# Gathering and put-back of tokens moved between half products, and four conditioning strips moved to an earlier stage

## Chip, cores and metric

One Trainium2 chip, one core. The metric is the device time of one execution in microseconds. The kernel is one program written out engine by engine (TensorE "PE", VectorE "DVE", ScalarE "ACT", GpSimd "POOL", SyncE "SP"), which meet only at semaphores.

## What is computed

256 tokens of 1024 features, float32. Two blocks in a row:

```
# first block
h = mixer(x)                 # four branches a (linear recurrence), b (gated delta rule),
                             # c (stick-breaking attention), d (gated linear attention);
merged = sum_n sigmoid(merge_in_n) * (y_n @ w_branch[n]);  h = merged @ w_out
x = layer_norm(2**0.25 * x + h)
scores -> best of 4 groups of 4 experts -> 2 experts of that group
y = sum_e combine[e] * ((silu(x @ w_gate[e]) * (x @ w_up[e])) @ w_down[e])
x = layer_norm(2**0.25 * x + y)
# second block, two layers
for i in 0, 1:
    mod = silu(c) @ ada_w[i] + ada_b[i]          # 1024 x 9216: shifts, scales, gates
    x = x + .5*g0*rmsnorm(swiglu(modulate(rmsnorm(x)), 1024 x 2752))
    x = x + g1*rmsnorm(attention_i(modulate(rmsnorm(x))))   # 0: sparse, 1: differential
    x = x + .5*g2*rmsnorm(swiglu(modulate(rmsnorm(x)), 1024 x 2752))
```

## The kernel before

**Weights.** SP loads every weight in units of 1 MB into a ring of six slots (L494 to L506). Unit n+6 is issued when unit n is released, by a count that PE or another engine raises after the last use of its slot. In the expert stage and in the feed-forward products each unit is split in two parts for precise products: ACT writes `w_hi` (`high_at`, L1703), DVE writes `w_lo` = weight less `w_hi` (`low_at`, L2409), and each product is three matmuls (`mm3`).

**First mixer.** The order of work on all engines comes from one list, `STEPS`. `d_gate` is the gates of branch d: eight matmuls on PE, then a chain of exponentials, logarithms and one scan on ACT and DVE (L1620, L2142) that ends in `d_q`; `d_attn` on PE (L850) waits for it. Between them stand merge steps 8 and 9. A merge step is the product of one 128-column gate tile and its branch tile; two of them share a unit of `w_in`, four a unit of `w_branch`, and DVE releases three units after every fourth step (L2292).

**Conditioning strips.** The product `silu(c) @ ada_w[i]` is a filler: 36 units a layer, in five quads, each a sum in one PSUM bank. A quad of eight units writes four rows at partitions 0, 32, 64, 96 (columns in four groups); the last quad, of four units, writes two. `p_ada` (L1009) makes one unit's share; when a quad is complete ACT copies it to `ada_row` (`ada_drain`, L1534) and POOL stores it (`store_quad`, L591). There is one `ada_row`, so a drain waits for the store before it. Layer one's strips (here number 0) lie in the first mixer and ahead of the experts; all 36 of layer two lie in sparse attention, as `fill(count)`: 3 + 5 before the index products, 8 within them, 8 behind them, and 2, 2, 2, 2, 1, 1, 1, 1 in the eight softmax iterations (L1380).

**Expert stage.** Tokens are sorted by group into five tiles of 128 slots; each tile passes its group's four experts, 20 runs in all. A run s is, on PE (`experts`, L1218): turn the hidden rows of run s-1 (`turn_hidden`, PSUM bank 4), two half products with `w_gate`, two with `w_up`, two with `w_down` of run s-1; a half product is 12 matmuls of 512 columns. In the run with e = 2 the next tile's tokens are gathered in four pieces (`gather`: eight small matmuls, taken out of PSUM by ACT's `sorted_rows`); in the run with e = 1 the finished tile is put back in four pieces (`scatter`: two matmuls, added to `acc`, which is `merged` in the profile, by DVE's `y_add`). All pieces of both use PSUM bank 7, one after the other. A put-back needs the tile's output split in two parts: ACT's `y_high`, then DVE's `y_low`, which raises `y_split`. DVE's order in a run is: `y_low` if putting back, `hid_lo` (raises `run_hT`), adds 0 to 2, `w_lo` of both `w_down` halves and of the next `w_gate` half 0, `run_h`, add 3, the other three `w_lo`.

## Time and profile before

| | us |
|---|---|
| median of 3 runs | 2211.09 (2205.53 to 2212.61) |
| profiled execution | 2211.7 |
| its span, first to last instruction | 2210.0 |
| PE busy | 2071.6 |
| DVE busy | 1188.6 |
| ACT busy | 903.0 |
| mean granted clock of PE | 0.945 |

The span is what the rows below add up to; 1.7 us of the profiled execution lie around it. PE's matmuls are recorded with their pipelined length, so that a busy PE says that matmuls follow each other, not at which rate: the distance between starts gives the rate. A time in brackets behind an instruction is the idle time of its engine before it, with what ended it. PEclk is the granted clock as a share of full speed: 1.00 is 2.4 GHz and 0.50 is 1.2 GHz.

### The profile page before, as it was taken

What the parts mean: (1) busy time and instruction counts of PE and PEld (TensorE: products, weight loads), DVE (VectorE), ACT (ScalarE), POOL (GpSimd) and SP (SyncE); (2) the same over time, 40 slices, a digit from 0 to 9 for tenths busy, and PEclk for the clock granted to TensorE, in tenths of its full rate; (3) what the DMA queues carried; (4) which work ended last, traced back from release to release, by engine and by line L of the source; (5) the groups of instructions that cost most, each with busy time, mean ns of one, the idle gap of its engine ahead of it and who ended that gap; (6) DMA issues with size and microseconds to landing.
All of it is one profiled execution on the core that took longest, in us unless ns stands there. A gap on an engine that the chain in (4) does not pass through costs nothing.

```text
span 2210.0 us, 29686 instructions
## 1 busy us (share of the span) xinstructions
PE 2071.6 (94%) x12013; PEld 1723.7 (78%) x12013; DVE 1188.6 (54%) x1686; ACT 903.0 (41%) x1300; POOL 60.7 (3%) x144
## 2 busy tenths in 40 slices
PE   8999989989979999998899997899999999879998
PEld 6777778787547777776899972489999999847997
DVE  2060353441269878878655646455566555455544
ACT  1132520111047776775443433443344335454333
POOL 5000000000000000000000000000000000000000
PEclk9999986987989999999899997999999999979999
DMA  6875220302589988898355679546655655403652
GB/s 220 283 265 180 94 98 17 103 13 95 203 332 336 327 324 309 311 355 302 129 183 184 199 274 419 194 139 205 195 185 173 199 180 191 153 20 114 205 194 95
DMA packets 207241, 441.81 MB, mean 200 GB/s; under 512 B 8108, under 2 KB 158732, under 8 KB 183584
## 3 DMA queue, kind: packets, MB, share of 16 engines
q1 hardware_dynamic: 201568, 424.70, 55.3%
q0 software_dynamic: 5568, 15.67, 2.1%
q8 instruction: 72, 1.18, 0.2%
q14 instruction: 33, 0.27, 0.0%
HBM read 439.14 MB, written 1.20 MB: 199 GB/s over the span
## 4 chain that ended last, share of the span: by engine, by line
PE 65%; DVE 6%; ACT 4%; DMA 4%; issue 1%; SPq 0%; ACTq 0%; DVEq 0%
PE P L672 64%; DMA ring<-in_ada_w 1%; DMA ring<-in_w_down 1%; ACT merged L1482 1%; DVE w_lo L2018 1%; DVE w_lo L2413 1%; DMA ring<-in_w_up 1%; ACT w_hi L1707 1%; DVE h L1971 1%; DMA ring<-in_w_gate 1%; DVE xs L1971 1%; DVE xs L1964 0%; ACT pT L1482 0%; DVE y_lo L1964 0%; ACT st L1482 0%
## 5 line engine op out<-in xcount | busy, mean ns | idle before, releaser
L672 PE MATMUL P<-x_parts,w_hi 128*128 128x256 f32 x2560 | 458.2, 281 | 2.1 <-DVE w_lo L2018 2.1
L672 PEld LDWEIGHTS P<-x_parts,w_hi 128*128 128x128 f32 x2560 | 399.0, 189 | 8.9 <-DVE w_lo L2018 2.8
L2018 DVE TENSOR_TENSOR w_lo<-ring,w_hi 128x1024 fp32r<-128x1024 f32 x302 | 351.5, 1220 | 79.6 <-ACT w_hi L1514 79.4
L672 PE MATMUL P<-w_hi,x_parts 128*128 128x256 f32 (+2 forms) x1504 | 375.7, 336 | 3.2 <-DVE w_lo L2413 3.2
L672 PE MATMUL P<-x_parts,w_lo 128*128 128x256 f32 x1280 | 361.2, 282 | 0.0
L1514 ACT ACTIVATE w_hi<-ring 128x1024 fp32r<-128x1024 f32 x302 | 297.4, 1050 | 52.1 <-DMA ring<-in_ffn_w_down 48.8
L2413 DVE TENSOR_TENSOR w_lo<-ring,w_hi 128x1024 fp32r<-128x1024 f32 x240 | 279.2, 1221 | 27.3 <-ACT w_hi L1707 25.4
L672 PEld LDWEIGHTS P<-w_hi,x_parts 128*128 128x128 f32 x1504 | 262.0, 194 | 32.4 <-issue 4.1
L1707 ACT ACTIVATE w_hi<-ring 128x1024 fp32r<-128x1024 f32 x240 | 240.5, 1052 | 105.2 <-DMA ring<-in_w_up 39.8
L672 PE MATMUL P<-xT,ring 128*128 128x256 f32 x1152 | 267.4, 389 | 4.5 <-ACT xT L1482 3.1
L672 PEld LDWEIGHTS P<-xT,ring 128*128 128x128 f32 x1152 | 222.6, 196 | 50.7 <-issue 20.2
L672 PEld LDWEIGHTS P<-x_parts,w_lo 128*128 128x128 f32 x1280 | 241.7, 189 | 0.0
L672 PE MATMUL P<-w_lo,x_parts 128*128 128x256 f32 (+2 forms) x752 | 238.4, 338 | 0.0
L672 PE MATMUL P<-w_hi,hid_hi 128*128 128x512 f32 x512 | 202.7, 396 | 1.7 <-DVE hid_lo L1964 1.4
L672 PE MATMUL P<-w_lo,hid_hi 128*128 128x512 f32 x512 | 204.2, 399 | 0.0
L672 PE MATMUL P<-w_hi,hid_lo 128*128 128x512 f32 x512 | 201.0, 392 | 0.0
L1698 ACT ACTIVATE silu<-P 128x256 f32<-128x256 f32 x88 | 33.7, 383 | 371.1 <-PE P L672 352.3
L2398 DVE TENSOR_TENSOR hid<-silu,P 128x256 f32<-128x256 f32 (+1 forms) x80 | 33.7, 421 | 251.1 <-ACT silu L1698 250.2
L672 PEld LDWEIGHTS P<-w_lo,x_parts 128*128 128x128 f32 x752 | 146.5, 195 | 12.7 <-issue 0.5
L672 PEld LDWEIGHTS P<-w_hi,hid_hi 128*128 128x128 f32 x512 | 96.4, 188 | 24.3 <-issue 1.9
L672 PEld LDWEIGHTS P<-w_hi,hid_lo 128*128 128x128 f32 x512 | 96.2, 188 | 22.7
L672 PEld LDWEIGHTS P<-w_lo,hid_hi 128*128 128x128 f32 x512 | 96.1, 188 | 17.9
(439 smaller groups left out, 2044.9 us busy)
## 6 DMA issues: line engine op xcount, KB each, us to landing
ring<-in_ada_w SPq DMA_DIRECT2D x72, 1024.0 KB, 8.9
ring<-in_ffn_w_gate SPq DMA_DIRECT2D x44, 1024.0 KB, 5.5
ring<-in_ffn_w_up SPq DMA_DIRECT2D x44, 1024.0 KB, 8.0
ring<-in_ffn_w_down SPq DMA_DIRECT2D x44, 1024.0 KB, 4.9
ring<-in_w_in SPq DMA_DIRECT2D x40, 1024.0 KB, 7.3
ring<-in_w_gate SPq DMA_DIRECT2D x40, 1024.0 KB, 4.9
ring<-in_w_up SPq DMA_DIRECT2D x40, 1024.0 KB, 4.9
ring<-in_w_down SPq DMA_DIRECT2D x40, 1024.0 KB, 5.1
```

The source lines that it names most:

```text
L672: return pe.matmul(o, l, r, start=start, stop=stop, **kw)
L1482: a.done(act.activation(o, i, fn, **kw), name)
L1514: act.activation(w_hi[:, slot, c:c + half], ring[:, slot, c:c + half], ACT.Copy).then_inc(sem("w_hi"), 1)
L1698: act.activation(silu[:, k % 2, :], P[:, k % 2, 0:S], ACT.Silu).then_inc(sem("silu"), 1)
L1707: act.activation(w_hi[:, n % R, c:c + UNIT // 2], ring[:, n % R, c:c + UNIT // 2], ACT.Copy).then_inc(sem("w_hi"), 1)
L1971: v.done(dve.scalar_tensor_tensor(out=o, in0=x, scalar=s, in1=y, op0=op0, op1=op1), name)
L2018: dve.tensor_tensor(w_lo[:, slot, c:c + half], ring[:, slot, c:c + half], w_hi[:, slot, c:c + half].bitcast(F32), ALU.subtract).then_inc(s ...
L2398: dve.tensor_tensor(x, silu[done:128, k % 2, :], P[done:128, k % 2, S:2 * S], ALU.mult).then_inc(sem("hid_part"), 1)
L2413: dve.tensor_tensor(w_lo[:, n % R, c:c + UNIT // 2], ring[:, n % R, c:c + UNIT // 2], w_hi[:, n % R, c:c + UNIT // 2].bitcast(F32), ALU.su ...
```

## The change

Five edits, of which the first two go together:

- **Four strips of layer two** (the last quad, now first in that layer's order) go from the softmax iterations of sparse attention into the first mixer, between `b_pre` and merge step 8, with their four 1 MB loads, one ACT drain and one POOL store. `d_attn` waits for the drain too, since it uses the same bank (7). The softmax iterations keep one strip each. `DRAINS` is the new order of drains over both layers.
- Waits, counts and the list of loads follow from that. The merge units of the ring are listed step by step, which is the same order as before apart from the four new ones.
- **Gathering** alternates between banks 7 and 4: pieces 0 to 3 stand behind half products gate 0, gate 1, up 0, up 1 as before, but piece q waits for the copy of piece q-2 and no more of q-1. Pieces 1 and 3 use the bank of `turn_hidden`, so piece 1 waits for `run_hT`, and the next run begins with a wait for all four copies. ACT copies pieces 1 and 2 one after the other behind `silu`, and piece 3 behind the next split.
- **Put-back** moves each piece one half product later: behind gate 1, up 0, up 1 and down 0.
- **DVE's order**: the adds 0, 1, 2, 3 stand behind `w_lo` of `w_down` half 0, of `w_down` half 1, behind `run_h`, and behind `w_lo` of the next `w_gate` half 1.

```diff
-QUADS = (2, 3, 4, 0, 1), (0, 1, 2, 3, 4)
-BANKS = (6, 7, 6, 0, 1), (6, 7, 6, 7, 6)
+QUADS = (2, 3, 4, 0, 1), (4, 0, 1, 2, 3)
+BANKS = (6, 7, 6, 0, 1), (7, 6, 7, 6, 7)
...
+NEXT_ADA = len(QUAD_UNITS[QUADS[1][0]])
+DRAINS = [(0, k) for k in range(EARLY)] + [(1, 0)] + [(0, k) for k in range(EARLY, ADA_QUADS)] + [(1, k) for k in range(1, ADA_QUADS)]
...
-STEPS += [("d_gate",), ("b_pre",), _MERGE[8], _MERGE[9], ("d_attn",), _MERGE[10], ("d_intra",)]
+STEPS += [("d_gate",), ("b_pre",)] + [("ada", n, 1) for n in range(NEXT_ADA)]
+STEPS += [_MERGE[8], _MERGE[9], ("d_attn",), _MERGE[10], ("d_intra",)]
...
             for k in range(EARLY):
                 store_quad(0, k)
+            store_quad(1, 0)
...
             def p_d_attn():
                 t.see("d_q")
                 pe.wait_ge(sem("y2"), 4)
+                pe.wait_ge(sem("ada_out"), DRAINS.index((1, 0)) + 1)
...
+                    if e == 3 and k + 1 < TILES:
+                        pe.wait_ge(sem("x_taken"), 4 * k + 8)
...
                         t.tell(wide_half("w_gate", s, 0, s % 2), "half_used")
                         if gathering:
                             if k:
                                 pe.wait_ge(sem("y_added"), 4 * k)
                             gather(k + 1, 0, 7)
+                        t.tell(wide_half("w_gate", s, 1, s % 2), "gate_out")
                         if scattering:
                             pe.wait_ge(sem("y_split"), k)
                             scatter(k - 1, 0, 7)
-                        t.tell(wide_half("w_gate", s, 1, s % 2), "gate_out")
+                        if gathering:
+                            pe.wait_ge(sem("run_hT"), s)
+                            gather(k + 1, 1, 4)
+                        t.tell(wide_half("w_up", s, 0, 2 + s % 2), "half_used")
+                        if gathering:
+                            pe.wait_ge(sem("x_taken"), 4 * k + 5)
+                            gather(k + 1, 2, 7)
                         if scattering:
                             pe.wait_ge(sem("y_added"), 4 * (k - 1) + 1)
                             scatter(k - 1, 1, 7)
-                        if gathering:
-                            pe.wait_ge(sem("x_taken"), 4 * k + 5)
-                            gather(k + 1, 1, 7)
-                        t.tell(wide_half("w_up", s, 0, 2 + s % 2), "half_used")
-                        if gathering:
-                            pe.wait_ge(sem("x_taken"), 4 * k + 6)
-                            gather(k + 1, 2, 7)
+                        t.tell(wide_half("w_up", s, 1, 2 + s % 2), "up_out")
                         if scattering:
                             pe.wait_ge(sem("y_added"), 4 * (k - 1) + 2)
                             scatter(k - 1, 2, 7)
-                        t.tell(wide_half("w_up", s, 1, 2 + s % 2), "up_out")
-                        if scattering:
-                            pe.wait_ge(sem("y_added"), 4 * (k - 1) + 3)
-                            scatter(k - 1, 3, 7)
                         if gathering:
-                            pe.wait_ge(sem("x_taken"), 4 * k + 7)
-                            gather(k + 1, 3, 7)
+                            pe.wait_ge(sem("x_taken"), 4 * k + 6)
+                            gather(k + 1, 3, 4)
...
                         t.tell(down_half(s - 1, 0), "half_used")
+                        if scattering and s < RUNS:
+                            pe.wait_ge(sem("y_added"), 4 * (k - 1) + 3)
+                            scatter(k - 1, 3, 7)
...
-                    fill((2, 2, 2, 2, 1, 1, 1, 1)[n])
+                    fill(1)
...
                         f(run_silu, P[:, s % 2, :], ACT.Silu, "run_silu")
                         if gathering:
-                            sorted_rows(k + 1, 1, 7)
+                            sorted_rows(k + 1, 1, 4)
+                            sorted_rows(k + 1, 2, 7)
                         if s + 1 < RUNS:
                             high_at(expert_at["w_gate", s + 1, 1])
                         if gathering:
-                            sorted_rows(k + 1, 2, 7)
+                            sorted_rows(k + 1, 3, 4)
...
-                        if scattering:
-                            for b in range(3):
-                                y_add(b, 7)
                     if 0 < s < RUNS:
                         low_at(expert_at["w_down", s - 1, 0])
+                        if scattering:
+                            y_add(0, 7)
                         low_at(expert_at["w_down", s - 1, 1])
+                        if scattering:
+                            y_add(1, 7)
...
                     if scattering:
+                        y_add(2, 7)
+                    if s + 1 < RUNS:
+                        low_at(expert_at["w_gate", s + 1, 1])
+                    if scattering:
                         y_add(3, 7)
```

## Rows read from the trace of the kernel before

**Rows 1.** The page, its parts 1 and 4: busy time, and the chain of waits.
```profile
PE 2071.6 (94%) x12013; PEld 1723.7 (78%) x12013; DVE 1188.6 (54%) x1686; ACT 903.0 (41%) x1300; POOL 60.7 (3%) x144
...
PE 65%; DVE 6%; ACT 4%; DMA 4%; issue 1%; SPq 0%; ACTq 0%; DVEq 0%
```

**Rows 2.** Waits of PE, 660 to 1032 us: waiter, releaser, us in total, times, longest.
```profile
PE P L672 <- DVE y_lo L1964: 6.5, 4, 2.9
PE P L672 <- ACT x_parts L1482: 4.1, 6, 1.6
```

**Rows 3.** Timeline of PE, expert stage: start, length, engine, line, operation, [idle before].
```profile
797.37 0.63 PE L1196 MATMUL P<-ident,hid 128*128 128x128 f32 x4
...
814.64 0.63 PE L1196 MATMUL P<-ident,hid 128*128 128x128 f32 x4
...
819.80 0.51 PE L672 MATMUL P<-y_hi,to_token 128*128 128x512 f32 x1 [1.77 <-DVE y_lo L1964]
...
820.38 0.39 PE L672 MATMUL P<-w_hi,x_parts 128*128 128x512 f32 x1
...
824.71 0.39 PE L672 MATMUL P<-y_hi,to_token 128*128 128x512 f32 x1
...
837.59 0.63 PE L1196 MATMUL P<-ident,hid 128*128 128x128 f32 x4
...
846.27 0.66 PE L672 MATMUL P<-to_slot,rows_hi 128*128 128x128 f32 x4 [1.58 <-ACT x_parts L1482]
```

**Rows 4.** Stretches: busy time of each engine, PEclk, DMA share, GB/s.
```profile
820.00:825.00 5.00, 5.00 (x16) 3.91 (x16) 1.16 (x2) 4.68 (x6) 0.00 (x0) 0.66 0.42 177
846.00:852.00 6.00, 5.73 (x24) 4.81 (x25) 6.00 (x6) 5.31 (x7) 0.00 (x0) 0.72 0.41 160
```

**Rows 5.** Waits of DVE 815 to 838 us; its timeline there and in the run behind.
```profile
DVE merged L1964 <- PE P L672: 6.9, 3, 4.1
...
818.34 1.41 DVE L1964 TENSOR_TENSOR y_lo<-P,y_hi 128x512 fp32r<-128x512 f32 x2
...
829.45 6.90 DVE L2413 TENSOR_TENSOR w_lo<-ring,w_hi 128x1024 fp32r<-128x1024 f32 x6
...
844.59 0.68 DVE L1964 TENSOR_TENSOR hid_lo<-P,hid_hi 128x512 fp32r<-128x512 f32 x1
```

**Rows 6.** Timeline of ACT, the run with gathering.
```profile
843.73 2.00 ACT L1707 ACTIVATE w_hi<-ring 128x1024 fp32r<-128x1024 f32 x2 [1.66 <-DMA ring<-in_w_down]
845.64 0.58 ACT L1482 ACTIVATE x_parts<-P 128x512 fp32r<-128x512 f32 x1
```

**Rows 7.** Timeline of PE and DVE, the gates' wait of the first mixer.
```profile
285.63 3.72 PE L672 MATMUL P<-xT,ring 128*128 128x256 f32 x16
...
294.37 1.89 PE L672 MATMUL P<-yT,ring 128*128 128x256 f32 x8
...
305.16 3.77 PE L672 MATMUL P<-gl_q,gl_k 128*128 128x128 f32 x16 [8.90 <-DVE gl_k L1964]
...
309.64 3.62 PE L672 MATMUL P<-xT,ring 128*128 128x256 f32 x16
...
308.11 0.42 DVE L1964 TENSOR_TENSOR merged<-merged,tmpm 128x256 f32<-128x256 f32 x1
```

**Rows 8.** Landing of the two loads of w_in issued at 284.0 and 284.5 us.
```profile
DMA to landing us min/median/max: 7.7/9.6/11.4
```

**Rows 9.** Timeline of PE, strips of a four-group quad and of the last quad.
```profile
150.76 1.04 PE L672 MATMUL P<-ring,cols 128*1 128x512 f32 x8
...
185.59 1.88 PE L672 MATMUL P<-ring,cols 128*1 128x512 f32 x8
```

**Rows 10.** Timeline of PE, sparse attention: last strip before the scores, first iterations.
```profile
1355.91 1.88 PE L672 MATMUL P<-ring,cols 128*1 128x512 f32 x8 [0.59 <-DMA ring<-in_ada_w]
...
1363.07 3.59 PE L672 MATMUL P<-ring,cols 128*1 128x512 f32 x16
```

**Rows 11.** Waits of ACT, the softmax iterations, 1366 to 1404 us.
```profile
ACT pT L1482 <- PE P L1387: 7.1, 6, 2.5
```

More of the change, by code:

```diff
@@ L168, in weight_loads @@
             out.append(projections.pop(0))
-        elif step == "ada":
-            ada(0, which[0])
-    for b in BRANCH_ORDER:
-        for half in range(2):
-            out.append((w_branch[b][:, half * 512:half * 512 + 512].rearrange("(t p) n -> p t n", p=128),
-                        4, 512, 128))
-            cols(w_in, C_MERGE + b * D + half * 512, 512)
+        elif step == "merge":
+            b, d = BRANCH_ORDER[which[0] // DT], which[0] % DT
+            if d % 4 == 0:
+                out.append((w_branch[b][:, d * 128:d * 128 + 512].rearrange("(t p) n -> p t n", p=128), 4, 512, 128))
+            if d % 2 == 0:
+                cols(w_in, C_MERGE + b * D + d * 128, 256)
+        elif step == "ada":
+            ada(which[1] if len(which) > 1 else 0, which[0])
     square(A["w_out"][0])
@@ L187, in weight_loads @@
                 if layer == 0:
-                    for n in range(ADA_UNITS):
+                    for n in range(NEXT_ADA, ADA_UNITS):
                         ada(1, n)
@@ L276, in quad_ends @@
     def quad_ends(layer, k):
-        return ADA_UNITS * layer + sum(len(QUAD_UNITS[q]) for q in QUADS[layer][:k + 1])
+        return sum(len(QUAD_UNITS[QUADS[l][j]]) for l, j in DRAINS[:DRAINS.index((layer, k)) + 1])
     with ctx:
@@ L449, in build @@
         SPARSE_WIDTHS = [256] * (A_IN // 256) + [A_IN % 256]
-        ATTENTION_UNITS = {"sparse": -(-A_IN // 256) + ADA_UNITS + D // 256, "differential": DIFF_IN // 256 + D // 256, "ffn": 0}
+        ATTENTION_UNITS = {"sparse": -(-A_IN // 256) + ADA_UNITS - NEXT_ADA + D // 256, "differential": DIFF_IN // 256 + D // 256, "ffn": 0}
         def out_bank(n):
@@ L593, in store_quad @@
                 rows, p = raw_rows(layer, QUADS[layer][k])
-                pool.wait_ge(sem("ada_out"), ADA_QUADS * layer + k + 1)
+                pool.wait_ge(sem("ada_out"), DRAINS.index((layer, k)) + 1)
                 pool.dma_start(rows, ada_row[0:p:32, :]).then_inc(sem("ada_stored"), 16)
             def load_modr(layer):
-                pool.wait_ge(sem("ada_stored"), 16 * ADA_QUADS * (layer + 1))
+                pool.wait_ge(sem("ada_stored"), 16 * (1 + DRAINS.index((layer, ADA_QUADS - 1))))
                 load(modr[:, layer, :], mod_raw[layer].rearrange("(p q) -> p q", q=128), "modr_here")
@@ L653, in _ @@
                 if n == 1:
-                    for k in range(ADA_QUADS):
+                    for k in range(1, ADA_QUADS):
                         store_quad(1, k)
@@ L1017, in p_ada @@
                     t.see("cond")
-                if d == 0 and k >= 2:
-                    pe.wait_ge(sem("ada_out"), ADA_QUADS * layer + k - 1)
+                if d == 0:
+                    earlier = [m for m, (l, j) in enumerate(DRAINS[:DRAINS.index((layer, k))]) if BANKS[l][j] == BANKS[layer][k]]
+                    if earlier:
+                        pe.wait_ge(sem("ada_out"), earlier[-1] + 1)
                 for dd in range(w.shape[1]):
@@ L1238, in experts @@
                         else:
-                            pe.wait_ge(sem("ada_out"), EARLY + s + 1)
+                            pe.wait_ge(sem("ada_out"), DRAINS.index((0, EARLY + s)) + 1)
                         t.tell(wide_half("w_gate", s, 0, s % 2), "half_used")
@@ L1330, in fill @@
                     for _ in range(count):
-                        k = filled[0]
+                        k = NEXT_ADA + filled[0]
                         filled[0] += 1
@@ L1536, in ada_drain, with a_ada @@
                 act.wait_ge(sem("ada_used"), quad_ends(layer, k))
-                if layer + k:
-                    act.wait_ge(sem("ada_stored"), 16 * (ADA_QUADS * layer + k))
+                before = DRAINS.index((layer, k))
+                if before:
+                    act.wait_ge(sem("ada_stored"), 16 * before)
                 p = 128 if QUADS[layer][k] < 4 else 64
                 f(ada_row[0:p, :], P[0:p, BANKS[layer][k], :], ACT.Copy, "ada_out")
-            def a_ada(n):
+            def a_ada(n, layer=0):
+                if layer:
+                    if n + 1 == NEXT_ADA:
+                        ada_drain(1, 0)
+                    return
                 for k in range(EARLY):
@@ L1769, in a_experts @@
                                 high_at(expert_at["w_up", s + 1, half])
-                        if gathering:
-                            sorted_rows(k + 1, 3, 7)
                         if s == RUNS - 1:
@@ L2473, in v_experts @@
                     if scattering:
+                        y_add(2, 7)
+                    if s + 1 < RUNS:
+                        low_at(expert_at["w_gate", s + 1, 1])
+                    if scattering:
                         y_add(3, 7)
                     if s + 1 < RUNS:
-                        low_at(expert_at["w_gate", s + 1, 1])
                         low_at(expert_at["w_up", s + 1, 0])
```

2 lines of the change are left out of this document (removed).

## The prediction

> **What bounds the kernel now.** I read the page first [rows 1]: PE is busy 94% of the span and makes up 65% of the chain that ended last; no other engine has more than 6%. So a part of the change is worth what it takes off PE's waits or PE's own work, and where PE waits for another engine, what is left of that engine's chain. Then I read, for the three places that the change touches, PE's waits and the timelines.
>
> In the expert stage PE waits for two things again and again [rows 2]: the first piece of a put-back for `y_low` (4 times, 6.5 us), the second or third piece of gathering for ACT's copy of the piece before (6 times, 4.1 us). An undisturbed run is 17.3 us, from one turn of the hidden rows to the next (797.37 to 814.64 [rows 3]). In the first mixer PE waits 8.9 us for the gates' chain [rows 7]. In sparse attention the last strips ahead of the scores wait for their loads [rows 10], and behind them ACT waits for PE's transposes [rows 11].
>
> **Put-back one half product later.** It removes the wait for `y_split` if that comes before gate 1 has ended. With T the start of the turn: in the run at T = 814.6 gate 0 ended at 818.0 and `y_low` at 819.75, that is T + 5.1 [rows 3, 5]. A half product takes 2.8 us (a run of 17.3 is six of them and a turn of 0.4), so the piece now stands at T + 6.0, and only the longest of the four waits (2.9 us, `y_low` at about T + 6.1) leaves 0.1. Gain 6.4 us.
>
> **The clock.** After the 1.77 us wait the same half product took 4.33 us from start to start (820.38 to 824.71) instead of 2.8 [rows 3]; PEclk is 0.66 in those 5 us and 0.72 in the 6 us behind the 1.58 us wait of a gathering [rows 3, 4]: each stands for a fall to 1.2 GHz. By the clock 0.34 of 5 us and 0.28 of 6 us are lost, 1.7 each; against the undisturbed half product it is 1.5 for the first. Without the waits I expect no fall: gain 3.1 us in these two places. The other waits had no fall behind them, not even the longest.
>
> The Trainium skill ("TensorE: Matmul & The Clock Gate", section "HAM oscillation") has a rule against this term: only idle gaps longer than these two throttle the clock again. By it the falls would have another cause and might stay. The rows show them right behind the waits.
>
> **Gathering over two banks.** Piece 1 no longer waits for the copy of piece 0. That copy was late because ACT first split a half of `w_down` whose load had come late: split 843.73 to 845.6, copy 845.64 to 846.22, PE's piece at 846.27 after 1.58 us [rows 3, 6]. With T = 837.6 [rows 3] the copy ended at T + 8.6; it is now due behind up 0, at T + 10.5. Gain 4.1 us. Added waits: piece 1 for `hid_lo` (DVE), which ended at 845.3, T + 7.7 [rows 5]; piece 1 stands at T + 6.9. With nothing else changed this would cost 0.8 us. But DVE was late there because it had stood 6.9 us ahead of three of the put-back's adds, waiting for PE's pieces [rows 5], which its new order takes away.
>
> **DVE's order.** A half split is 1.15 us (6.90 for six [rows 5]), so a run costs DVE 12 times 1.15 plus 0.7 for `hid_lo` and 0.7 for `run_h`, 15.2 us, and a put-back 1.4 for `y_low` [rows 5] and four adds of 0.7: 19.4 us, against PE's 17.3 plus four pieces of 0.5 to 0.6, 19.4. DVE is level with PE in that run, but has 2.1 us to spare in each of the others. Following its queue from `y_split` at T + 4.8 (mean of four): `hid_lo` 5.5, half 0 of `w_down` 7.8, add 0 8.5, half 1 10.8, add 1 11.5, next `w_gate` 13.8, `run_h` 14.6, add 2 15.3. PE wants the splits of `w_down` at T + 13.1 and add 2, for the last piece, at T + 15.9. So nothing waits in three of the four, and about 0.7 us in the latest. The remaining splits and add 3 end at T + 22.9. The next run begins at T + 19.4, so its `hid_lo` ends 4.2 us into it, ahead of the 6.9 at which gathering wants it. What is queued behind a late last piece is down 1, then the turn; nobody else. I allow 1.3 us for both new waits.
>
> ACT stands still between the copies of pieces 1 and 2, from about T + 11 to PE's piece 2 at T + 11.4, with the next split behind it; that split fed a product of the next run, 9 us later. The wait for four copies at the turn is met by T + 16 against T + 20.5. Both cost nothing; if ACT were 4 us late in these runs they would cost the excess.
>
> Expert stage: 6.4 + 3.1 + 4.1 - 1.3 = **12.3 us** gained. Bounds: 13.8 with no new wait, 5 if new waits of 1 us stand at each of the eight places.
>
> **Strips in the softmax iterations.** Eight strips become PE's savings: one of 1.8 us at the low clock in iteration 0 (3.59 for two [rows 10]), three of 0.95, and in the last four iterations a strip of the last quad (1.88) becomes one of a four-group quad (1.04 recorded, 0.95 from start to start) [rows 9], 0.9 each: 8.3 us of PE. But ACT is the next bound: it waits 7.1 us for the transposes in six iterations [rows 11]. In the first (2.5 us) only 1.8 go, in the last (2.0) only 0.9; the other four (together 2.6) go whole. 1.8 + 2.6 + 0.9 = 5.3, less 0.3 for the first strip behind the index products, which now waits for a drain that ACT makes after its last relu: **5.0 us**. The start of the iterations does not move: 24 strips stand ahead of the scores before and after, and the last of them waits for its load [rows 10]. Bounds 2 (DVE's softmax chain comes next) and 7.1.
>
> **The same strips in the gates' wait.** Four strips of 1.82 us (the record of 1.88 less overlap [rows 9]) are 7.3 us for a wait of 8.9 [rows 7]. Merge steps 8 and 9 ran from 285.6 to 296.3, 10.6 us; with the strips ahead they run from 292.9 to 303.6, if the loads are there. The first three strips are loaded early; the fourth shares an issue with the two units of merge step 8. The last of three such loads landed 11.4 us after its issue at 284.5, at 295.9 [rows 8]. So the two steps end between 303.6 and 306.5, against 305.16: cost 0 to 1.3. Against that `d_attn`, 16 small matmuls, took 3.77 us at the low clock after the wait [rows 7]; at full clock they take about half, a gain of up to 1.8, of which 1.1 is usable, since merge step 10 waits for DVE's `merged` at 308.53 [rows 7] and began at 309.64. ACT's drain and POOL's store lie in time that both have free; who waits for the store is the next drain, hundreds of us later. I take **0.3 us** gained, bounds -3 (clock falls while the loads are waited for) and +1.1.
>
> **Sum.** 12.3 + 5.0 + 0.3 = 17.6 us. The profiled execution (2211.7, span 2210.0) goes to 2194.1; it lies 0.6 above the median, so the median goes from 2211.1 to **2193.5 us**. About 0.3%, 6.6 us, is what a measurement of this kernel can tell from no change.
>
> **Rivals.**
> - New waits take half of the expert gain: PE arrives earlier, and ACT and DVE, bound to the loads, do not follow. For it: ACT splits only just after landing [rows 6]. Against: both have slack by the queue above. Expert stage 6, rest 3: 2202. Chance 0.17; a quarter of it lies above 2204.5.
> - The clock's falls stay or move elsewhere, as by the page's rule: 3.1 us less, 2196.6. Chance 0.12.
> - The gates' wait costs: steps 8 and 9 run at the low clock behind late loads and end 4 to 5 us late: 2198. Chance 0.1.
> - Sparse attention gives nothing, since DVE and ACT set its iterations at once: 2198.5. Chance 0.08.
> - Slower: `hid_lo` for piece 1 and add 2 for the last piece. PE now meets DVE at eight places where it met it at four. If DVE comes 2.6 us later at each than the queue above says, that is 21 us and the clock falls behind four of them, 6 us: 27 against 18.9, so 2219. With the 6 us it decides from 1.6 us a place. Against: DVE's idle time of 6.9 us in each put-back goes. Chance 0.05.
> - The forecast, with new waits under 2 us: chance 0.48, by itself 2190 to 2197.
>
> Range 2187 to 2204: the low end is the upper bounds of all three parts (13.8, 7.1, 1.1) and 2 us for a clock that stays up elsewhere, the high end the first rival. Faster 0.87, same 0.08, slower 0.05.
>
> **What would show it.** Right: no PE wait for `y_low` in the middle of the stage; gathering's waits under 0.5 us; DVE's waits for the put-back (`merged` from PE) gone; ACT's wait for transposes near 2 us; PE idle at the gates under 2 us; `d_attn` at 305. Wrong: PE waiting for `hid_lo` or `merged` at the new places; PE waiting for `w_lo` in a run after a gathering; steps 8 and 9 behind a load; the softmax iterations as long as before, with ACT's wait now on `nmax`.

## Result, and the profile after

The changed kernel takes 2186.05 us (median of 4 runs, 2181.51 to 2187.24) against 2209.48 of the kernel before in the same session (2205.53 to 2212.61): 0.9883 of its time, 95% interval 0.9866 to 0.9900. That is 23.4 us less, where 17.6 was forecast, and 0.95 us below the low end of the range. The sign was right, the size too small. The forecast started from 2211.09, the median of three runs of the kernel before; with a fourth run that median is 2209.48, so 1.6 of the 7.4 us between the forecast time and the measured one are a shift of the base. By the ratio the gain is 22 to 30 us. The profiled execution took 2185.02, its span is 2183.2.

The page after, its parts 1 and 4, against [rows 1]: PE has 6 us less of busy time and 27 us less of span.

```profile
PE 2065.7 (95%) x12013; PEld 1714.5 (79%) x12013; DVE 1189.5 (54%) x1686; ACT 903.8 (41%) x1300; POOL 60.7 (3%) x144
...
PE 68%; DVE 6%; ACT 3%; DMA 2%; issue 1%; SPq 0%; ACTq 0%; DVEq 0%
```

**Expert stage.** The waits of PE after, 654 to 1010 us, against [rows 2] (waiter, releaser, us in total, times, longest). Of the 6.5 us for `y_lo` 0.3 are left, the 4.1 for `x_parts` are gone, and what is recorded at the new places is 0.5 (the last two lines). The first two lines stand in both kernels: 1.41 us for `hid_lo` right behind the last of the 20 turns and 0.84 for `hid` ahead of them (before, at 1032.1 and 663.9 us).

```profile
PE P L679 <- DVE hid_lo L1978: 1.4, 1, 1.4
PE P L1206 <- DVE hid L1985: 0.8, 1, 0.8
PE P L679 <- DVE y_lo L1978: 0.3, 1, 0.3
PE P L679 <- DVE merged L1978: 0.2, 1, 0.2
```

The timeline of PE after, in the first put-back run: turn, last matmul of gate 1, the first matmul of the piece, next turn. The piece follows 0.23 us behind the matmul ahead of it, and the run takes 19.06 us from turn to turn.

```profile
730.66 0.63 PE L1206 MATMUL P<-ident,hid 128*128 128x128 f32 x4
...
736.44 0.40 PE L679 MATMUL P<-w_hi,x_parts 128*128 128x512 f32 x1
736.67 0.39 PE L679 MATMUL P<-y_hi,to_token 128*128 128x512 f32 x1
...
749.72 0.63 PE L1206 MATMUL P<-ident,hid 128*128 128x128 f32 x4
```

The whole stage from the first turn to the twentieth, as stretches (length, busy time of PE, PEld, DVE, ACT and POOL, PEclk, DMA share, GB/s), after and then before:

```profile
658.10:1008.00 349.90, 349.36 (x1605) 286.36 (x1606) 311.58 (x295) 259.96 (x289) 2.19 (x4) 1.00 0.95 344
```
```profile
663.90:1030.10 366.20, 355.25 (x1605) 287.83 (x1606) 311.05 (x295) 259.21 (x289) 2.19 (x4) 0.99 0.91 330
```

It is 16.3 us shorter. PE hardly stands still any more, no low clock is left in the stage (PEclk 1.00; the falls before are in [rows 4]), and DVE's idle time in the adds ([rows 5]) has become idle time ahead of splits, in which nothing waits for it.

**Gates' wait.** The timeline of PE after, against [rows 7] (idle time before in brackets):

```profile
280.88 1.99 PE L679 MATMUL P<-lrT,wup 16*128 16x256 f32 x8
282.80 7.03 PE L679 MATMUL P<-ring,cols 128*1 128x512 f32 x32
291.58 3.69 PE L679 MATMUL P<-xT,ring 128*128 128x256 f32 x16 [1.75 <-DMA ring<-in_w_in]
...
302.33 2.05 PE L679 MATMUL P<-gl_q,gl_k 128*128 128x128 f32 x16
304.21 1.04 PE L868 MATMUL P<-ident,d_kd 128*128 128x128 f32 x8
305.85 3.69 PE L679 MATMUL P<-xT,ring 128*128 128x256 f32 x16 [0.60 <-DVE merged L1978]
```

The 8.9 us of idle are filled: four strips, then 1.75 us of waiting for the load that the prediction named, then the two merge steps. `d_attn` takes 2.05 us instead of 3.77. PEclk is 1.00 from 292 to 306 us, where it was 0.63 from 296 to 310 before.

**Softmax iterations of sparse attention**, as stretches from the first scores to the product with `w_out`, cut at the start of the fourth copy of `pT`: after, then before.

```profile
1334.60:1356.70 22.10, 17.65 (x112) 8.19 (x108) 14.16 (x25) 13.29 (x47) 0.00 (x0) 0.71 0.90 357
1356.70:1382.80 26.10, 18.12 (x117) 8.15 (x117) 11.58 (x16) 15.75 (x41) 0.57 (x1) 0.87 0.61 198
```
```profile
1357.70:1381.70 24.00, 19.91 (x144) 8.43 (x140) 14.65 (x25) 13.86 (x48) 0.57 (x1) 0.81 1.02 416
1381.70:1406.50 24.80, 18.49 (x116) 8.14 (x117) 11.09 (x16) 15.75 (x41) 0.57 (x1) 1.00 0.82 292
```

The first half gained 1.9 us and the second lost 1.3: together 0.6, where 5.0 was forecast. In the second half the clock is at 0.87 where it was at 1.00.

Where the 26.8 us between the two spans lie, from the starts of the same instructions:

| stretch | before | after | gained | forecast |
|---|---|---|---|---|
| start to the `lrT` product | 283.7 | 280.9 | 2.8 | 0 |
| to merge step 10 | 25.9 | 25.0 | 1.0 | 0.3 |
| to the first turn of the experts | 354.3 | 352.2 | 2.1 | 0 |
| to the 20th turn | 366.1 | 349.9 | 16.3 | 12.3 |
| to the first scores | 327.6 | 326.7 | 1.0 | 0 |
| softmax iterations | 48.8 | 48.2 | 0.6 | 5.0 |
| to the end | 803.5 | 800.4 | 3.1 | 0 |

The three stretches that hold the edits gained 17.9 us together, about what was forecast, and not where it was forecast: the expert stage gave 4.0 more and the softmax iterations 4.4 less. That the two nearly cancel is luck. The other 9.0 us lie in four stretches from which nothing was moved.

### The profile page after: what moved, and what is told of

Read it like the earlier page. It is cut to its first block, busy times and chain, and to the rows that moved or that the text cites. A ratio compares the mean times of both kernels' runs of the same rounds, so it can differ in the third digit from the quotient of the medians.

```text
span 2183.2 us, 29690 instructions
## 1 busy us (share of the span) xinstructions
PE 2065.7 (95%) x12013; PEld 1714.5 (79%) x12013; DVE 1189.5 (54%) x1686; ACT 903.8 (41%) x1300; POOL 60.7 (3%) x144
## 4 chain that ended last, share of the span: by engine, by line
PE 68%; DVE 6%; ACT 3%; DMA 2%; issue 1%; SPq 0%; ACTq 0%; DVEq 0%
PE P L679 67%; DMA ring<-in_ada_w 1%; ACT merged L1494 1%; DVE w_lo L2032 1%; DVE h L1985 1%; DVE xs L1985 1%; DVE xs L1978 0%; ACT pT L1494 0%; PE P L1206 0%; DMA ring<-in_w_up 0%; DVE w_lo L2427 0%; ACT st L1494 0%; ACT big L1494 0%; DMA ring<-in_w_gate 0%; PE P L1322 0%
## 5 line engine op out<-in xcount | busy, mean ns | idle before, releaser
L1526 ACT ACTIVATE w_hi<-ring 128x1024 fp32r<-128x1024 f32 x302 | 297.4, 1050 | 51.4 <-DMA ring<-in_ffn_w_down 48.5
L679 PEld LDWEIGHTS P<-w_hi,hid_hi 128*128 128x128 f32 x512 | 96.5, 188 | 22.5 <-DVE hid_lo L1978 1.6
```

What stands on the lines that cost most here:

```text
L679: return pe.matmul(o, l, r, start=start, stop=stop, **kw)
L1526: act.activation(w_hi[:, slot, c:c + half], ring[:, slot, c:c + half], ACT.Copy).then_inc(sem("w_hi"), 1)
```

## Experiments

**The two parts apart.** `strips_only` is the changed kernel with the expert stage of before; `experts_only` is the kernel before with that stage alone changed; both kernels ran once more beside them. The edits are those of the diff.

> The four strips moved, the expert stage as before. Theory 1 (softmax iterations gain almost nothing because the granted clock falls more often there once PE has less to do): the gates give 1 us, the stretch before the scores 0 to 1.5, the iterations 0.5 to 1.5; in all 2 to 4 us, ratio 0.998 to 0.999, and the low-clock time between the first scores and the last copy is longer than in the kernel before. Theory 2 (the forecast's 5.3 us is right and the changed kernel's profile was an unlucky one in this stage): 5 to 6 us, ratio 0.9975, iterations of 44 us instead of 48.8. Either way the 20 expert runs keep their lengths (22 us with gathering, 20.5 to 23 with put-back).

> Gathering over two banks and the later put-back, the strips as before. Theory 1 (each wait removed was worth its recorded idle time, some tenths more for draining and refilling PE, and the clock's falls behind two of them): 16 us, 2193, ratio 0.9927; runs with put-back 19.1 us, with gathering 20.7 us, all alike. Theory 2 (forecast: 12.3 us; the rest of the 16.3 us seen in the changed kernel was luck of the clock): 2197, ratio 0.9944, with two or more of these eight runs longer than 21 us.

> The kernel before, unchanged, for a second profile. If the 2.8 us that the changed kernel was ahead at the first gate product (280.9 against 283.7 us), and the 2.7 us between sparse attention and the end, are the phase of the clock and no work of the change, then this profile shows the gate product at another time than 283.7 (between 280 and 285) and other places of low clock in the feed-forward stages; if they come from the change, it shows 283.7 and the same places again. The waits of the expert stage are the same in kind: four for y_lo, six for x_parts, 10 to 12 us in all.

> The changed kernel, unchanged, for a second profile. Same question from the other side: if the clock's phase is free, the first gate product stands at another time than 280.9. The expert runs are 19.1 and 20.7 us in every execution, and the softmax iterations take 44 to 49 us: near 44 if the falls of the clock there are luck, near 48 again if they are brought about by the missing strips.

Measured: `strips_only` 0.9967 (0.9947 to 0.9987), 7.3 us (3 to 12). `experts_only` 0.9925 (0.9897 to 0.9952), 16.6 us (11 to 23). The parts add up to 23.9 us; the whole is 25.9 by its ratio (22 to 30) and 23.4 by the medians. For `experts_only` its first theory, 16 us, holds; `strips_only` lies above both of its theories (2 to 4, and 5 to 6), but its interval reaches into both. Against the forecast 16.6 stand for 12.3 and 7.3 for 5.3; both intervals reach down to the forecast, so it is the lengths of the stages that say where the shortfall lies. `before_again` took 2214.07 and `after_again` 2188.69.

The expert stage, from the first turn to the 20th: 366.1, 361.5 and 369.6 us in the three profiles with the old stage (before, `before_again`, `strips_only`), 349.4, 349.9 and 351.3 with the new one. The old stage differs from one execution to the next by 8 us, the new one by 2: what scattered were its waits and the falls of the clock (2, 0 and 3 in these three). A forecast from one execution carried that scatter with it.

**The expert stage taken apart.** `putback_only` is the kernel before with the later pieces and DVE's order; `gather_only` is the kernel before with gathering over two banks. `old_adds` is the changed kernel with

```
+                        if scattering:
+                            for b in range(3):
+                                y_add(b, 7)
                     if 0 < s < RUNS:
                         low_at(expert_at["w_down", s - 1, 0])
-                        if scattering:
-                            y_add(0, 7)
                         low_at(expert_at["w_down", s - 1, 1])
-                        if scattering:
-                            y_add(1, 7)
...
```

and `y_add(3, 7)` right behind `run_h`.

> Put-back later and DVE's new order; gathering as before (one bank), strips as before. Theory: a wait in the middle of the stage costs PE more than its recorded idle time, because the matmul ahead of it no longer overlaps the next, and the new waits cost nothing. Then each of the first three put-back runs takes 19.1 us and the last 19.1 to 20.4, the gathering runs stay at 22.0 or more, and the time falls by 8 to 10 us, where the prediction's own terms for this part (6.4 of waits, 1.5 for one fall of the clock, less half of 1.3) give 7.2. Rival: the gathering runs, too, become shorter by 1 us each, because DVE no longer stands in the adds: then this part alone gives 12 or more and gathering over two banks is worth 4 or less. Second rival: DVE is late for the pieces without the second bank; put-back runs of 20 us or more.

> Gathering over two banks only; put-back, DVE's order and strips as before. Theory: gathering runs of 20.7 to 21.0 us (22.0, 22.0, 24.2, 22.1 before), put-back runs as before (20.5 to 23), gain 6 to 8 us. The prediction's rival for piece 1: DVE still stands in the adds of the run before, so hid_lo is late by 0.8 us for it, in three of the four gathering runs (none is preceded by a put-back in the first): runs of 21.5 us or more, gain 4 us or less.

> The changed kernel with DVE's order of before: adds 0 to 2 right behind hid_lo, add 3 right behind run_h. Theory: the new order is a needed part of the change. DVE then stands in its adds until piece 2 has been made, at 13 us behind the turn; add 0.7 and the split of w_down 1.15 put that split at 14.9, where PE wants it at 13.0. Each of the four put-back runs becomes 1.9 to 2.2 us longer (21 us), and up to 1.6 more where the clock falls behind that wait: 8 to 14 us longer than the changed kernel, 2194 to 2203. Rival: the later pieces and the second bank do all the work, and DVE's order matters as little as its 54% of busy time suggests: no put-back run over 19.4, time within 2 us of the changed kernel.

Measured: `putback_only` 0.9943 (0.9910 to 0.9976), 12.6 us (5 to 20); `gather_only` 0.9963 (0.9943 to 0.9984), 8.2 us (3.5 to 13); `old_adds` 2213.2 in one execution, no faster than before. The run lengths, from turn to turn, say it more sharply. For `putback_only` the put-back runs below give 8.9 us, as expected (8 to 10); the 12.6 agree with them within the interval. For `gather_only` the gathering runs give 4.1, as its rival said (4 or less), and not the 6 to 8 of its theory; the 8.2 leave both open.

| | put-back runs | gathering runs |
|---|---|---|
| before | 20.5, 23.0, 20.6, 22.5 | 22.0, 22.0, 24.2, 22.1 |
| `putback_only` | 19.1, 19.1, 19.1, 20.5 | 21.9, 22.0, 22.1, 22.0 |
| `gather_only` | 20.7, 21.2, 20.6, 24.0 | 21.2, 21.7, 21.7, 21.7 |
| after | 19.1, 19.1, 19.1, 20.4 | 21.0, 20.7, 20.7, 20.7 |
| `old_adds` | 25.4, 24.2, 24.1, 25.4 | 21.0, 20.7, 20.7, 20.7 |

The later pieces do their work without the second bank, and the gathering runs do not shorten by them (the 24.2 of before holds a fall of the clock): the first rival of `putback_only` falls. With the second bank alone three of four gathering runs stay 0.9 us above the changed kernel's. The row of PE for `gather_only`, piece 1 in such a run, shows the wait that the prediction had named and put at 0.8:

```profile
766.88 0.66 PE L672 MATMUL P<-to_slot,rows_hi 128*128 128x128 f32 x4 [0.66 <-DVE hid_lo L1965]
```

With DVE's old order every put-back run is 5 to 6 us longer than in the changed kernel, where 1.9 to 2.2 and at most 1.6 for the clock had been expected, and longer than in the kernel before. DVE's timeline in the first of them, and the matmul of PE that waits (the first of down 0):

```profile
741.67 0.69 DVE L1978 TENSOR_TENSOR merged<-merged,P 128x512 f32<-128x512 f32 x1 [0.87 <-PE P L679]
744.95 0.69 DVE L1978 TENSOR_TENSOR merged<-merged,P 128x512 f32<-128x512 f32 x1 [2.59 <-PE P L679]
748.21 0.69 DVE L1978 TENSOR_TENSOR merged<-merged,P 128x512 f32<-128x512 f32 x1 [2.58 <-PE P L679]
748.94 6.90 DVE L2427 TENSOR_TENSOR w_lo<-ring,w_hi 128x1024 fp32r<-128x1024 f32 x6
```
```profile
751.44 0.77 PE L679 MATMUL P<-w_hi,hid_hi 128*128 128x512 f32 x1 [3.33 <-DVE w_lo L2427]
```

DVE stands 6.0 us between its adds, and the split that PE wants comes behind them. A half of `w_down` is two of these six instructions, 2.3 us; my expectation had counted one, 1.15, and so was short. The clock falls at each of the four waits, too: of the 5 to 6 us 3.3 are the recorded wait, and the stage holds 20.5 us at 1.2 GHz. The order of DVE's adds is a needed part of the later put-back: without it the change gains nothing.

**Softmax iterations.** Two strips in each of the last four and none in the first:

```
-                    fill(1)
+                    fill((0, 0, 0, 0, 2, 2, 2, 2)[n])
```

> The changed kernel with its eight remaining strips of the softmax iterations in the last four of them (0, 0, 0, 0, 2, 2, 2, 2 instead of one each). Theory: the iterations are bound by PE at 1.2 GHz in the first three, and in the last four the clock falls again behind PE's waits for ACT as soon as PE has one strip less than before. Without strips the first four become 3 to 4 us shorter (22.0 to about 18.5 from the first scores to the fourth copy of pT), and with two in each of the last four no stretch of low clock stands there and they take 24.8 us as in the kernel before: 43 to 44 us in all against 48.1, so 4 to 5 us faster than the changed kernel in an execution like its profiled one, 2181 to 2185 on a chip on which that has 2188.7. Rival: the iterations follow ACT's and DVE's chain whatever the strips do: 48 us in all. Second rival: two strips in an iteration wait for their loads, which are issued one for each strip done: PE waits for DMA in the last four, 50 us or more.

Measured: 0.9894 (0.9859 to 0.9930), no better than the changed kernel: 2192.75 us, where 2181 to 2185 had been expected. The iterations took 47.3 us, the first four 21.0 instead of the 18.5 expected. The stretches of `late_fill`, and PE in it after the fourth iteration:

```profile
1337.80:1358.80 21.00, 14.32 (x80) 8.77 (x76) 13.93 (x25) 13.29 (x47) 0.00 (x0) 0.62 0.53 219
1358.80:1385.10 26.30, 20.19 (x148) 8.52 (x148) 11.81 (x16) 15.66 (x40) 0.56 (x1) 0.94 0.77 284
```
```profile
1357.14 0.65 PE L1399 MATMUL P<-ident,pr 128*128 128x128 f32 x4 [0.58 <-DVE pr L1978]
1359.42 0.65 PE L679 MATMUL P<-pT,proj 128*64 128x256 f32 x4 [1.63 <-ACT pT L1494]
1360.00 1.65 PE L679 MATMUL P<-kT,qT 64*128 64x256 f32 x8
```

In the first four PE was at 1.2 GHz for 15.9 us where the changed kernel has 12.7 (PEclk 0.62 for 0.71). The low stretch begins ahead of the scores and is 20.5 us long in both; whether the missing strips carried it further into the iterations, or it only began later, this run does not tell. Behind the waits of 0.58 and 1.63 us the next scores are again at the low level (1.65 us instead of 1.13). Most of the work taken from PE was paid back by the clock.

`zero_late` tests that from the other side: the changed kernel with an extra strip of products with a column of zeros in each of the last four iterations.

```
-                    for j in range(w.shape[2] // 512):
-                        x = mm(P[32 * j:32 * j + 1, BANKS[layer][k], :], cols[:, V_C + d + dd:V_C + d + dd + 1],
-                               w[:, dd, j * 512:j * 512 + 512], start=d + dd == 0, stop=d + dd == 7)
+                    for zero in ((True, False) if extra and d + dd else (False, True) if extra else (False,)):
+                        for j in range(w.shape[2] // 512):
+                            x = mm(P[32 * j:32 * j + 1, BANKS[layer][k], :], causal_neg[:, 0:1] if zero else cols[:, V_C + d + dd:V_C + d + dd + 1],
+                                   w[:, dd, j * 512:j * 512 + 512], start=d + dd == 0 and not zero, stop=d + dd == 7 and not zero)
...
-                    fill(1)
+                    fill(1, n >= 4)
```

> The changed kernel with one extra strip of zero products in each of the last four softmax iterations: eight matmuls with a column of zeros, added to the same sum, which nothing needs and which load nothing. PE has there the work that it has in the kernel before. Theory: the clock falls late in the iterations because PE has too little to do beside its waits for ACT's pT; with the extra work no low stretch stands in the last four, and they take the 24.8 us of the kernel before (from the fourth pT copy to the product with w_out), no more than the 26.1 that the changed kernel needed with one strip less. Rival: the falls have another cause and stay; then the extra 3.8 to 7 us of work come on top of the 26.1 in part, 28 us or more.

Measured, the stretches of `zero_late`:

```profile
1342.80:1364.70 21.90, 17.46 (x112) 8.18 (x108) 14.15 (x25) 13.28 (x47) 0.00 (x0) 0.72 0.90 359
1364.70:1389.50 24.80, 18.55 (x148) 8.28 (x149) 11.59 (x16) 15.72 (x41) 0.57 (x1) 1.00 0.61 206
```

32 more matmuls, and the last four iterations take 24.8 us instead of 26.1, at a PEclk of 1.00 instead of 0.87. The place where it turns, in the changed kernel and in `zero_late`:

```profile
1362.93 1.09 PE L679 MATMUL P<-pT,proj 128*64 128x256 f32 x8 [1.91 <-ACT pT L1494]
1363.95 1.70 PE L679 MATMUL P<-kT,qT 64*128 64x256 f32 x8
1365.58 1.89 PE L679 MATMUL P<-ring,cols 128*1 128x512 f32 x8
```
```profile
1370.94 1.09 PE L679 MATMUL P<-pT,proj 128*64 128x256 f32 x8 [1.05 <-ACT pT L1495]
1371.96 1.13 PE L679 MATMUL P<-kT,qT 64*128 64x256 f32 x8
1373.03 1.04 PE L679 MATMUL P<-ring,causal_neg 128*1 128x512 f32 x8
```

The added strip fills 0.86 us of the wait, and scores and strips behind it stay at full clock. The rest of the kernel is outside this test: its time as a whole, 2200 in one execution, is above the changed kernel's, by longer stretches ahead of the experts (383.0 us from the `lrT` product to the first turn, against 377 to 381 in the other profiles of the new mixer) and behind sparse attention, where its code is the same. It is one execution, and one of the five profiles without the added strips (`old_adds`, below) had no fall there either.

`after_third` is the changed kernel once more.

> The changed kernel once more, beside the two below on the same chip. Theory: its softmax iterations (first scores to the first product with w_out) take 44.1 to 44.3 us in an execution in which PE is at 1.2 GHz for under 9 us of them, and 48.0 to 48.2 where it is so for 19 us; nothing in between is tied to the loads. Its ratio to the kernel before is 0.987 to 0.990. Rival: the length of the iterations goes by something else than the low clock, for instance by when their loads land; then a length near 44 comes with 19 us of low clock, or one near 48 with 9.

Measured: 0.9891 (0.9859 to 0.9923). The iterations by profile, with the time at 1.2 GHz within them from the records of the granted clock (us: length, of it at 1.2 GHz):

| | whole | first four | last four |
|---|---|---|---|
| as before: before, `before_again`, `experts_only`, `putback_only` | 48.5 to 48.8, 8.5 to 9.2 | 23.7 to 24.0, 8.5 to 9.2 | 24.8, 0 |
| as before: `gather_only` | 46.3, 1.9 | 21.5, 1.7 | 24.8, 0.3 |
| one strip each: after, `after_third`, `strips_only` | 48.0 to 48.2, 19.4 to 19.5 | 22.0, 12.5 to 12.7 | 26.1, 6.8 |
| one strip each: `after_again` | 44.1, 7.0 | 19.3, 3.4 | 24.8, 3.6 |
| one strip each: `old_adds` | 44.2, 8.6 | 20.7, 8.6 | 23.5, 0 |

At the same 8.5 to 9 us of low clock, all in the first four, one strip each is 4.4 us shorter (`old_adds` against the first row), which is nearly the forecast of 5.0: 3.1 in the first four and 1.3 in the last. In three of five profiles the clock took 4 us of it back: 2.6 in the last four, by two falls, and 1.3 in the first four, by a low stretch that began ahead of the scores and reached 4 us further into them. The falls in the last four came in four of these five profiles and in none of the five with the strips of before, but for the last 0.3 us of `gather_only`. `zero_late` shows the same from the other side. For the longer low stretch of the first four no run shows a cause. The length goes with the low clock, and the same kernel shows both.

**ACT's wait inside the iterations.** ACT's wait for the transposes fell to 5.0 us (7.1 before [rows 11]), and its wait for the product behind `pT`, which the prediction had not named, rose from 7.0 to 8.4. Over all iterations the first is 2.7 us in `after_again` and 2.3 in `old_adds`, where the clock was low for less of them, near the 2 that the prediction named. The waits of ACT after, 1343 to 1381 us, and the second of them before, 1366 to 1404:

```profile
ACT oT L1494 <- PE P L679: 8.4, 7, 2.2
ACT pT L1494 <- PE P L1399: 5.0, 4, 1.7
```
```profile
ACT oT L1482 <- PE P L672: 7.0, 7, 1.3
```

`late_copy` makes the copy of the product (`head_rows`, which holds the removed lines) only behind the next exponentials on ACT; `late_copy_between` moves the strip, too, behind the transposes (PE):

```
+                    if n:
+                        head_rows(n - 1)
                     for j in range(i + 1):
                         a.see("pt")
...
-                    a.see("o_psum")
-                    f(oT[:, 2 * hg:2 * hg + 2, i * 128:i * 128 + 128],
-                      P[:, 4 + n % 2, 0:S].rearrange("p (a b) -> p a b", b=128), ACT.Copy, "o_out")
+                head_rows(7)
```
```
-                    fill(1)
                     t.see("p_ready")
...
                         t.tell(x, "pt")
+                    fill(1)
                     pe.wait_ge(sem("pt_out"), t.sent["pt"])
```

> The changed kernel with ACT's copy of an iteration's product (oT) behind the exponentials of the iteration after the next instead of ahead of them. ACT waited 9.7 us in eight places for that product in the changed kernel. Theory: ACT's chain bounds the iterations wherever PE is at full clock, 4.0 us each in the first four (four exponentials 2.1, pT 0.6, wait 0.8, oT 0.4) and 5.4 in the last; without the wait they take 3.4 to 3.6 and 4.6 to 4.8, and PE, which comes next with 3.4 and 4.1, has less time to stand still. 3 to 6 us faster than the changed kernel. Rival: PE is at 1.2 GHz for longer as soon as it is the later one, or DVE's chain (1.2 + 1.2 + 0.35 + 1.2 us an iteration) takes over: within 1.5 us of the changed kernel.

> The kernel late_copy with the strip of each iteration between PE's transposes and the product that waits for ACT's copy of them, instead of ahead of the transposes. Theory: PE's waits for pT (9.5 us in eight places in the changed kernel) lie behind the strip, of 0.95 us at full clock, so that 0 to 0.2 us are left of most, and ACT gets the transposes a strip earlier; as PE's idle goes, so do the falls of the clock within the iterations: 2 to 4 us faster than late_copy, iterations of 38 to 41 us. Rival: the clock is low there for what lies ahead of the iterations (waits for the strips' loads) and a strip at 1.2 GHz, 1.8 us, now stands in the chain from pT to oT: no gain over late_copy, or a loss of up to 3 us.

Measured: `late_copy` 0.9883 (0.9852 to 0.9913), iterations of 41.7 us; `late_copy_between` 0.9866 (0.9836 to 0.9896), 2185.5 us against 2190.4 of `after_third` on the same chip, iterations of 41.1. The iterations are 2.4 to 7 us shorter than the 44.1 to 48.2 of the changed kernel; 38 to 41 had been expected of the second. Of the 3 to 6 us expected of `late_copy` the span of its profiled execution shows 4.5 (2183.6 against 2188.1) and its median 1.4; of the 2 to 4 us more expected of `late_copy_between` they show 4.0 and 3.5. The intervals of the ratios overlap. The stretches of `late_copy_between` and its waits of PE (9.5 us for `pT` in the changed kernel):

```profile
1334.90:1355.70 20.80, 17.30 (x112) 8.48 (x108) 14.28 (x25) 13.25 (x46) 0.00 (x0) 0.71 0.95 371
1355.70:1376.00 20.30, 15.20 (x117) 7.53 (x117) 11.46 (x16) 15.83 (x42) 0.57 (x1) 1.00 0.70 221
```
```profile
PE P L679 <- ACT pT L1494: 3.0, 3, 1.2
PE P L1398 <- DVE pr L1985: 2.6, 3, 1.2
```

No stretch of low clock is left in the last four, in either kernel. The low clock at the start of the iterations (0.71) is still there. It begins ahead of the scores, among strips that wait for their loads (1.6, 1.3, 0.6 and 0.6 us in the changed kernel); whether these waits bring it, no run here tried. Of the two edits only the first shows a gain of its own in the iterations (41.7 from 44 to 48); the second's 0.6 us is too small to tell.

## Why the prediction fell short

Two steps of the sum failed, in opposite directions. The first took the recorded idle time of PE's waits in the expert stage as their full price; it made the forecast too small and carried the time out of the range. The second held the clock as it was in the softmax iterations; it made the forecast too large.

- **Put-back's waits: right in mechanism, the step that priced them failed.** The term of 6.4 was too small. The 6.4 was the recorded idle time. The four runs of before are 10.3 us longer than four of 19.07, with 1.5 for the clock's fall in one of them; 2.3 us, 0.6 a run, are in neither. The rows of PE before, in the first of them:

```profile
740.71 0.39 PE L672 MATMUL P<-w_hi,x_parts 128*128 128x512 f32 x1
742.00 0.50 PE L672 MATMUL P<-y_hi,to_token 128*128 128x512 f32 x1 [0.90 <-DVE y_lo L1964]
742.34 0.39 PE L672 MATMUL P<-y_lo,to_token 128*128 128x512 f32 x1
...
752.13 0.40 PE L672 MATMUL P<-y_lo,to_token 128*128 128x512 f32 x1
752.60 0.47 PE L672 MATMUL P<-w_hi,hid_hi 128*128 128x512 f32 x1
```

  Without a wait the piece starts 0.23 behind the matmul ahead of it; here it starts 1.29 behind, and the next 0.34 behind the piece. That is 1.17 us for a recorded 0.90, since the matmul ahead is recorded with its pipelined length of 0.39. Another 0.24 lies, unrecorded, ahead of down 0 in the same run (752.13 to 752.60). Measured 10.3 for waits and clock, forecast 7.9. The sum's own length of an undisturbed put-back run, 19.4, would have given 9.0 against the four runs of before (86.6); it was not set against them.
- **Gathering: right in mechanism, 4.1 and 1.5 too small.** Measured 7.1 in place of 5.6, in part for the same reason: six recorded waits, and a lost overlap at each (in the second gathering run the piece starts 0.93 us behind the matmul ahead of it for a recorded 0.54, and 0.23 without a wait). The wait for `hid_lo` was 0.7 us with DVE's old order and nothing with the new one, as worked out.
- **New waits: 1.3 allowed, 1.3 measured,** 0.5 of it recorded. It is what the last put-back run of after is longer than the other three (20.36 against 19.07). DVE's queue as worked out held; this run, for which 0.7 had been worked out, was the one late place. So the stage gave 10.3 + 7.1 - 1.3 = 16.1 of the measured 16.3, where 12.3 was forecast. The rival that half of the gain is eaten, and the slower one, fall with it.
- **The clock's falls went with the waits.** No stretch of low clock lies in the stage in any of the eight profiles with the new expert stage, nor in `putback_only`. In the five others (before, `before_again`, `strips_only`, `gather_only`, `old_adds`) there are 2, 0, 3, 1 and 4. The longest waits of `before_again`, 1.6 us, had none behind them, so a wait of this length may or may not bring one. That the falls stay, the second rival, is refuted for the stage. The rule of the Trainium skill ("TensorE: Matmul & The Clock Gate", section "HAM oscillation"), by which only idle gaps longer than these throttle the clock again, would have kept the 3.1 us out of the gain; the rows of this case speak against it.
- **Softmax iterations: the step that held the clock constant failed.** The prediction took PE's 8.3 us, capped by ACT's 7.1 of waiting, and held the clock as it was. Measured 0.6 in the profiled execution, 1.6 between the means of five profiles each. The mechanism was there (4.4 us at equal low clock). But with a strip less PE waits longer for ACT's `pT` (9.5 us in all instead of 7.4; at the place shown 1.91 us, where one strip more leaves 1.05), and in the last four iterations the clock fell behind such waits in four of five profiles, 1.3 us each time. The waits alone do not decide it: `old_adds` has 10.1 us of them and no fall there. The rival that DVE and ACT set the pace at once came near the time (0.6 us), by luck: it names the wrong cause, for the same code took 23.5 us in the last four in `old_adds` and 26.1 in after.
- **Gates' wait: 0.3 forecast, 1.0 measured in that stretch**, within the bounds of -3 and +1.1. With the strips ahead of them steps 8 and 9 end just when the gates' chain does (`d_attn` starts 21.4 to 21.5 us behind it in both; 23.0 in `late_fill` and `after_third`, where the clock fell behind the wait for the load, 1.97 us in the first). What was gained is `d_attn` at full clock; between the means of five profiles with the old order and nine with the new one it is 0.8 us (25.9 and 25.1). The 2.1 us behind it were not in the sum. From merge step 10 to the first turn the old kernels take 352.7 to 358.3 us (mean 355.4) and the new ones 352.2 to 358.0 (mean 353.7), and after has not less but more low clock there than before (116 us, 113 before): no run shows that the change gains anything in that stretch.
- **Outside the edits** lie 2.8 us ahead of them, the 2.1 behind the gates, 1.0 ahead of the scores and 3.1 at the end. From kernel to kernel the first of these stretches is 279.1 to 283.7 us and the last 800 to 809; the kernel before itself reached the `lrT` product at 283.7 us and, in `before_again`, at 281.6. So most of these 9.0 us can be scatter of the single profiled execution. Without them the profiles give 17.9 us, where the medians gave 23.4. In the same way `strips_only` gained 7.3 us (3 to 12) in the medians, and its two stretches show 2.4 between means of profiles (1.6 and 0.8). Where the rest lies stays open.

So the sum failed in two terms of opposite sign: the expert stage was worth 16 us and not 12.3, and the softmax iterations 0.6 to 4.4 and not 5.0; the mixer gave 1.0 and not 0.3. The low end of the range took 13.8 for the expert stage as its upper bound (its terms, 6.4, 3.1 and 4.1, make 13.6). It held the recorded idle time for the full price, and there the range was too narrow: the stage passed it by 2.5 us. The miss of the range by 0.95 us is smaller than the shift of the base.

## What to carry to other kernels

Price a removed wait of a busy TensorE by the distance between starts, against the same run where it does not wait; the recorded idle time was too little at each wait looked at (1.17 for 0.90 at one; 10.3 us for 6.5 over four runs, 1.5 of it a fall of the clock). Work taken from a stage in which PE alternates with another engine is worth its time only if the clock stays up: look at the granted clock behind the waits that it leaves, and shorten these waits (with ACT's copy later the last four iterations took 21.5 us, with no fall). When an engine's adds are moved later, move them in that engine's own queue as well; the order of DVE alone was worth 22 us here, falls of the clock included (four put-back runs of 99.1 us in place of 77.6).

## What the runs showed of the hardware

- Adding 32 matmuls that nothing needs made four iterations 1.3 us shorter (24.8 for 26.1), by a granted clock of 1.00 for 0.87. That is one execution; without the added matmuls three profiles took 26.1 and two others 24.8 and 23.5.
- The same kernel, in the same stretch, takes 44.1 or 48.2 us, with PE at 1.2 GHz for 7.0 or for 19.5 us of it.
- A strip of a four-group quad takes 1.04 us and one of the last quad, with two groups, 1.88 [rows 9]; four of the latter in the gates' wait took 7.03.
